# A hybrid decoder step on one core: the gate's up-unit formed before the value's, the short convolution's outer factor multiplied last, weight loads in the matching order

## The reference

```
def causal_dwconv(v, buf, w):                      # width 3, along the sequence
    cat = jnp.concatenate([buf, v], axis=1)
    return sum(w[k] * cat[:, k:k + seq] for k in range(3)), cat[:, -2:]

def short_conv_mixer(h, buf, w_in, conv_w, w_out):
    gate_b, gate_c, v = split(h @ w_in, 3)
    conv_out, new_buf = causal_dwconv(gate_c * v, buf, conv_w)
    return (gate_b * conv_out) @ w_out, new_buf

def conv_ffn(h, buf, w_up, conv_w, conv_b, w_down):
    conv_out, new_buf = causal_dwconv(h @ w_up, buf, conv_w)
    val, gate = split(conv_out + conv_b, 2)
    return (jax.nn.gelu(gate) * val) @ w_down, new_buf
```

## Time and profile before

| | |
|---|---|
| median of 3 runs | 2626.61 us (2625.88 to 2627.5) |
| the profiled execution | 2623.26 us, of which its span 2621.5 us |
| mean granted TensorE clock | 0.971 |
| PE busy | 2459.7 us (94%), 15940 matmuls |
| PEld busy | 2345.7 us (89%) |
| DVE busy | 1591.4 us (61%) |
| POOL busy | 1088.2 us (42%) |
| ACT busy | 644.4 us (25%) |
| DMA | 200.96 MB, mean 77 GB/s |

### The profile page before, as it was taken

The page is one execution under the profiler, slowest core; times in us unless marked ns, Lnnn a source line. Parts: engine busy times, 40 slices in busy tenths (PEclk is TensorE's granted clock), DMA queues, the critical chain, the costliest instruction groups (busy, mean ns, idle before and its releaser), DMA issues.

```text
span 2621.5 us, 40061 instructions
## 1 busy us (share of the span) xinstructions
PE 2459.7 (94%) x15940; PEld 2345.7 (89%) x15940; DVE 1591.4 (61%) x2224; ACT 644.4 (25%) x1255; POOL 1088.2 (42%) x770
## 2 busy tenths in 40 slices
PE   5977779998999999999998999988999999999996
PEld 2766669997999999999987999987999999999995
DVE  7766882356566666666665454656566666666665
ACT  2222341135222222212224101015312222122223
POOL 3576003455544443443444444424743444344330
PEclk8889889999999999999999999999999999999998
DMA  8666753100111111111111111101111111111102
GB/s 314 252 221 242 249 190 131 42 29 28 58 49 49 49 41 49 46 44 49 49 33 33 62 38 52 49 25 33 57 41 49 49 45 44 49 44 46 41 25 72
DMA packets 79071, 200.96 MB, mean 77 GB/s; under 512 B 27328, under 2 KB 35264, under 8 KB 77760
## 3 DMA queue, kind: packets, MB, share of 16 engines
q1 hardware_dynamic: 61952, 155.83, 17.4%
q10 hardware_dynamic: 16960, 42.80, 4.7%
HBM read 177.47 MB, written 21.14 MB: 76 GB/s over the span
## 4 chain that ended last, share of the span: by engine, by line
PE 63%; DVE 14%; issue 7%; DVEq 5%; POOL 4%; ACT 4%; POOLq 1%; DMA 1%; ACTq 0%; SPq 0%
PE bank L602 12%; PE bank L604 12%; PE bank L603 12%; PE bank L837 7%; PE bank L839 7%; PE bank L838 7%; DVEq L1846 3%; DVE ROWS L1845 3%; DVE ROWS L1844 2%; PE bank L880 1%; DVE ROWS L1848 1%; POOL WL L424 1%; DVE ROWS L1853 1%; DVE GL L1831 1%; ACT XRAW L1191 1%
## 5 line engine op out<-in xcount | busy, mean ns | idle before, releaser
L602 PE MATMUL bank<-HH,WH 128*128 128x344 f32 x3024 | 976.8, 323 | 15.2 <-ACT ROWS L1249 10.7
L603 PE MATMUL bank<-HL,WH 128*128 128x344 f32 x3024 | 969.2, 320 | 0.0
L604 PE MATMUL bank<-HH,WL 128*128 128x344 f32 x3024 | 969.0, 320 | 0.0
L422 POOL TENSOR_TENSOR WH<-RAW,ZERO 128x1024 fp32r<-128x1024 f32 x188 | 365.6, 1945 | 1149.1 <-PE bank L604 606.5
L602 PEld LDWEIGHTS bank<-HH,WH 128*128 128x128 f32 x3024 | 571.7, 189 | 30.2 <-issue 23.9
L603 PEld LDWEIGHTS bank<-HL,WH 128*128 128x128 f32 x3024 | 571.3, 189 | 0.0
L604 PEld LDWEIGHTS bank<-HH,WL 128*128 128x128 f32 x3024 | 571.2, 189 | 0.0
L424 POOL TENSOR_TENSOR WL<-RAW,WH 128x1024 fp32r<-128x1024 f32 x188 | 532.6, 2833 | 14.8
L1700 DVE SCALAR_TENSOR_TENSOR X<-bank,MOD,X 128x344 f32<-128x344 f32 (+1 forms) x480 | 274.1, 571 | 324.3 <-PE bank L839 224.1
L837 PE MATMUL bank<-GH,WH 128*128 128x344 f32 x1248 | 409.2, 328 | 14.8 <-DVE X L1724 14.7
L839 PE MATMUL bank<-GH,WL 128*128 128x344 f32 x1248 | 401.5, 322 | 0.0
(11 more groups left out here) (309 smaller groups left out, 2344.7 us busy)
## 6 DMA issues: line engine op xcount, KB each, us to landing
RAW<-in_wstream SPq DMA_DIRECT2D x188, 512.0 KB, 3.3
ADA<-in_wada ACTq DMA_DIRECT2D x40, 1024.0 KB, 5.2
s_pack<-PKA SPq DMA_DIRECT2D x8, 1344.0 KB, 4.6
PKB<-s_pack SPq DMA_DIRECT2D x12, 512.0 KB, 6.0
PKB<-s_pack SPq DMA_DIRECT2D x8, 576.0 KB, 5.0
XRAW<-in_xT SPq DMA_DIRECT2D x8, 516.0 KB, 16.6
X<-in_xT SPq DMA_DIRECT2D x1, 4128.0 KB, 13.5
out_yT<-X SPq DMA_DIRECT2D x3, 1376.0 KB, 5.6
```

Source lines behind the costliest of these rows:

```text
L422: pool.tensor_tensor(WH[:, slot, :], RAW[:, slot % 2, :], bc(ZERO[:, :], [128, 1024]), ALU.add).then_inc(s_hi, 1)
L602: pe.matmul(o, wh, hh, start=k == 0, stop=False)
L603: pe.matmul(o, wh, hl, start=False, stop=False)
L604: m = pe.matmul(o, wl, hh, start=False, stop=k == KC - 1)
```

## The change

In each ConvFFN chunk the gate's unit comes first and the value's second, on SP, PE, ACT and DVE alike. ACT waits for the split of the chunk before only in front of the value's rows. s_conv is signalled after the gate's taps, in front of the value's, and a drain stands in front of the product. In the last chunk the takes of items 0 and 1 move from between the two convolutions to the middle of the value's (behind its first tap and the drain). In the short convolution the units come in the order C, v, b. DVE begins when C and v have been copied and waits for b in front of the last product; ACT waits for s_g2 in front of the first chunk alone. The host's stream keeps its order: SP picks the units of a group in the new order with an offset, and its loop is written by phase.

```diff
+GATE_FIRST = (1, 0, 3, 2)
+B_LAST = (1, 2, 0, 4, 5, 3)
-            def load_unit(n, slot):
+            def load_unit(n, slot, at=0):
                 sp.wait_ge(s_unit, n - 1)
-                sp.dma_start(RAW[:, slot, :], wstream[bass.ds(n, 1), :, :].rearrange("a p n -> p (a n)"))\
+                sp.dma_start(RAW[:, slot, :], wstream[bass.ds(n + at, 1), :, :].rearrange("a p n -> p (a n)"))\
                     .then_inc(s_raw[slot], 16)
+            def load_phase(n0, order, groups):
+                up_n = len(order)
+                def ups(n):
+                    for q in range(up_n):
+                        load_unit(n + q, q % 2, order[q] - q)
+                ups(n0)
+                with sp.Fori(0, groups - 1) as a:
+                    ups(n0 + up_n + (up_n + 2) * a)
+                    for q in range(2):
+                        load_unit(n0 + 2 * up_n + (up_n + 2) * a + q, q)
+                for q in range(2):
+                    load_unit(n0 + up_n + (up_n + 2) * (groups - 1) + q, q)
-            with sp.Fori(14, NU // 2) as a:
-                for b in range(2):
-                    load_unit(2 * a + b, b)
+            load_phase(N_F0, GATE_FIRST, FC // 2)
+            load_phase(N_SC, B_LAST, 4)
+            load_phase(N_F1, GATE_FIRST, FC // 2)
...
# ACT, ffn_rows
-                act.wait_ge(s_g2, rows_done)
-                for vg in range(2):
+                for i, vg in enumerate((1, 0)):
+                    if first or vg == 0:
+                        act.wait_ge(s_g2, rows_done)
-                        act.wait_ge(s_up, 3 * u + 2 * t + vg + 1 if first else 3 * (u + vg) + t + 1)
-                        b = BK[3 * vg + t]
+                        act.wait_ge(s_up, 3 * u + 2 * t + i + 1 if first else 3 * (u + i) + t + 1)
+                        b = BK[3 * i + t]
...
# ACT, short_conv
-                        if q == 0:
-                            act.wait_ge(s_g2, c0 + c)
+                        if q == 0 and c == 0:
+                            act.wait_ge(s_g2, c0)
-                            dst = (T1[:, TH * t:TH * (t + 1)], U0[:, 2 + TH * t:2 + TH * (t + 1)],
-                                   U1[:, 2 + TH * t:2 + TH * (t + 1)])[q]
+                            dst = (U0[:, 2 + TH * t:2 + TH * (t + 1)], U1[:, 2 + TH * t:2 + TH * (t + 1)],
+                                   T1[:, TH * t:TH * (t + 1)])[q]
...
# DVE, ffn_conv
-                for vg in range(2):
-                    if vg and between:
-                        between()
+                for i, vg in enumerate((1, 0)):
-                    dve.wait_ge(s_ev, 3 * (u0 + 1 + vg) + 6 * cc)
+                    dve.wait_ge(s_ev, 3 * (u0 + 1 + i) + 6 * cc)
                     stt(Tr[:, 0:SEQ], Ur[:, 1:1 + SEQ], cw[1], Tr[:, 0:SEQ], M, A)
                     stt(Tr[:, SEQ:NT], st[1], cw[1], Tr[:, SEQ:NT], M, A)
                     fence()
+                    if vg == 0 and between:
+                        between()
                     stt(Tr[:, SEQ:NT], st[0], cw[0], Tr[:, SEQ:NT], M, A)
                     last = stt(Tr[:, 0:SEQ], Ur[:, 0:SEQ], cw[0], Tr[:, 0:SEQ], M, A)
-                last.then_inc(s_conv, 1)
+                    if vg == 1:
+                        last.then_inc(s_conv, 1)
             def ffn_product(cc, gel0):
+                fence()
                 dve.wait_ge(s_gelu, gel0 + 1 + cc)
...
# DVE, short_conv
-                    dve.wait_ge(s_ev, 3 * (u0 + 3 * c + 3))
+                    dve.wait_ge(s_ev, 3 * (u0 + 3 * c + 2))
...
+                    dve.wait_ge(s_ev, 3 * (u0 + 3 * c + 3))
                     tt(T0, T0, T1, M).then_inc(s_prod, 1)
```

More of the change, by code:

```diff
@@ L393, in _ @@
             sp.dma_start(STF[:, :, :, :], stf[0]).then_inc(s_late, 16)
-            with sp.Fori(0, 4) as a:
+            with sp.Fori(0, 3) as a:
                 for b in range(4):
                     load_unit(12 + 4 * a + b, b % 2)
-            with sp.Fori(14, NU // 2) as a:
-                for b in range(2):
-                    load_unit(2 * a + b, b)
+            load_phase(N_F0, GATE_FIRST, FC // 2)
+            load_phase(N_SC, B_LAST, 4)
+            load_phase(N_F1, GATE_FIRST, FC // 2)
             sp.wait_ge(s_y2, 1)
```

## The result

| | before | changed |
|---|---|---|
| median of 4 runs | 2627.06 us (2625.88 to 2628.66) | 2602.28 us (2599.6 to 2607.21) |
| profiled execution, of which span | 2623.26, 2621.5 us | 2607.21, 2605.4 us |

The ratio is 0.9907 with a 95% interval of 0.989 to 0.9925: 24.8 us faster by the medians. The profiled execution happens to be the slowest of the four, 4.9 us over their median, while that of the kernel before lies 3.8 under its own.

The account below looks back on a forecast made before the run. PE was taken as the bound, busy 594.67 of 600 us in the first ConvFFN's loop. Gains of 15.0 (loops) and 9.7 (short convolution's tail) less 2.0 (ConvFFN tails) gave 22.7 us, so 2603.9 us, range 2597 to 2614.

Parts of the forecast that it names:

- ConvFFN loops, 15.0 us: Both ConvFFN loops: 18 PE stalls for the copy of an up third vanish, a gain of 15.0 us.
- the bad bound: Short convolution's tail: the last product takes up to 2.54 us in place of 1.23 if it meets POOL.
- the 2.7 us of lower clock: Short convolution's tail: the 7.0 us PE wait lowers the clock for 6.2 us, costing 2.7 us more.
- Short convolution's tail, 9.7 us: Short convolution's tail: the 7.0 us PE wait and the lower clock behind it go, a gain of 9.7 us.
- ConvFFN tails, a loss of 1 us each: Both ConvFFN tails: the value's first taps delay the first take, costing about 1 us each, 2.0 in both.
- The wait of 0.7 before item 6: ConvFFN tails: second, 0.7 us part of PE's split wait, for the second pair of taps and take 2.
- the rival that was given 0.1: ConvFFN tails: the clock falls, 2.7 us more lost in each, gain only 17.3 us, 2609.3; chance 0.1.
- 4.4 us for both tails with POOL out of the way: ConvFFN tails: without POOL the item 6 stall vanishes, gaining 4.4 us; rival total 29.3 us, 2597.3, chance 0.1.
- Loads and drains: Whole kernel: SP's extra address arithmetic is hidden; 44 new drains cost about 0.2 us each on DVE, already counted.
- the rival that PE's waits are made up for later: The change does nothing that counts, as in layer norms behind the tails: 2624 to 2627 us; chance 0.04.
- the one in which the loop's stall stays: ConvFFN loops: the chain is no shorter where it counts; gain 7.7 us, 2618.9; chance 0.07.
- The slower rival: ConvFFN loops: DVE's chain grows by two more meetings with POOL per group, 24 us slower, 2651; chance 0.04.

Follow-up runs that it names:

- the two experiments: The changed kernel with only GELU hidden behind the value's taps, and with only the wait for the previous chunk's split moved: 2601.21 and 2601.49 us.
- the part alone: Short convolution's new unit order alone, ConvFFNs as in the kernel before: 2615.83 us, ratio 0.9962 to the kernel before.
- the kernel with only the hidden GELU: The changed kernel, but ACT waits for the previous chunk's split in front of the gate's rows, as before the change: 2601.21 us.
- the later split: The changed kernel, but POOL splits each ConvFFN's last unit only after DVE has taken tail item 3: 2604.37 us, ratio 0.9912 to before.
- the constants had been moved as well: The changed kernel with POOL's last split later and the layer norm's five constants formed before the last two chunks' work: 2596.52 us, ratio 0.9885.

## Why the prediction came out

Predicted 2603.9 us (2597 to 2614), measured 2602.28.

- **ConvFFN loops, 15.0 us**: measured 7.32 + 7.35 = 14.7, and the mechanism as written: taps at the same times, the product at their end, the copy free 2.5 us earlier, where the forecast had 2.3 (746.5 in place of 748.78). What the prediction did not say is that each half of the edit would have done alone; the two experiments showed it, and the prediction's own rows gave it (0.95 and 1.23 against 0.79).
- **Short convolution's tail, 9.7 us**: measured 10.0. The idle time and the lower clock after it are both gone, though the product did take the 2.54 us of the bad bound. That the 2.7 us of lower clock belong to the wait is shown by the part alone: with the order of before the granted clock in this tail is 0.92, with the new one 1.00.
- **ConvFFN tails, a loss of 1 us each**: +1.06 in the first, right as a figure, but by luck. Its parts were mis-sized. The wait before item 4 was 2.21 (forecast 2.3), since the taps took 4.2 us as worked out from the loop's rows. The wait of 0.7 before item 6 did not come in the first tail (in the second it was 0.13); instead the clock fell there, the rival that was given 0.1, 15 matmuls in 3.5 us, which is 3.5 - 15 x 0.158 = 1.1 us at that place and not 2.7. What the taps cost and what the clock costs come apart in the kernel with only the hidden GELU, whose first tail has the same order of taps and takes but a clock of 1.00: 58.87 us. So of the 1.06, 0.53 are the taps' and 0.53 the clock's (the rest of the 1.1 falls where that kernel waits 0.13 and 0.23 us for DVE before items 6 and 8, and the changed one does not). In the second tail the clock stayed up behind the same 2.21 us, and the cost at the full clock is again 0.53 us (73.49 against 72.96, above), not 1. There the stretch to the end reads -0.3 because the clock had fallen in the kernel before, for 1.0 us: the prediction read from the earlier trace rows that the wait of 2.02 us leaves the clock up, which is so in the first tail and was not in the second.
- **POOL's part in the tail**: the taps were long because of POOL, shown by the later split (1.28 and 0.22 us). The gain that the prediction put on it, 4.4 us for both tails with POOL out of the way, was not there until the constants had been moved as well; then it was 2.4 + 2.2 = 4.6 us. What that price had left out is that the split, moved away from the taps, lands on other work of DVE.
- **Loads and drains**: at no cost, as said; the drain in front of the product is 0.14 us.
- The layer norms behind the tails kept what they were given, so the rival that PE's waits are made up for later is out; likewise the one in which the loop's stall stays. The slower rival needed two more meetings with POOL in each group. The odd chunk's taps, behind the takes, took the same 16.7 us. The even chunk's did not: in a group before, one of them met POOL (3.06 us for 1.28), in a group of the changed kernel two do (8 sample columns in 1.86 us for 0.21 and in 2.29 for 0.23). From the first ConvFFN's third up unit to its first tail item DVE is busy 459 us where it was 432, with as many instructions, and PE has no wait for it. So "the same times as now" held for the chunk that PE had waited for, and not for DVE as a whole.

The median lies 1.6 us under the forecast; the profiled stretches sum to 24.2 us where the forecast has 22.7, and of the 1.5 us between them 1.3 are the second tail: 0.5 for the taps in place of 1.0, the 1.0 of lower clock in the kernel before, and 0.2 the other way behind the wait for ACT.

## What to carry to other kernels

When an engine that is the bound waits for the end of a chain, work out how much too long the chain is before shortening it: 0.8 us were missing here, and either of two edits gave them. A factor that is only multiplied in at the end should be computed last, so that everything before it is done while it is being computed; this pays where the chain's end is exposed, in a tail. In a tail served by one busy engine, moving its tasks about mostly moves the wait (0.3 and 0.6 us were won by it here). Find the take that PE waits for and clear what stands in front of it: the same five constants were worth nothing while the wait stood in front of them and 1.7 to 2.1 us once it stood behind. After each move, see what a split of another engine now falls beside.

## What the hardware showed unexpectedly

- A wait of about 2 us does not decide PE's clock by its size: behind the same 2.21 us it fell in the changed kernel's first tail (15 matmuls in 3.5 us) and stayed in the second. Over the six kernels with that wait in both tails it fell in 5 of 12; in the first tail it fell in four of the six and stayed in two, which run the same code there (59.40 and 58.87 us). A gain or loss of 0.5 to 1 us read from one profiled tail may be only this.
- Stretches with the same code take two lengths. The last GLU units with the layer norm and the first two units take 103.54 to 103.57 us or 105.22 to 105.27 us in the twelve traces of this study, with the same granted clock of 0.95 in the two kinds (before 103.5, changed 105.2). The windows of the traces tell them apart: the lower level comes equally long, but in the short kind behind a PE wait of 2.3 us for X, where the slower matmuls only eat into the next wait, for ACT in the layer norm (1.6 us), and in the long kind behind that wait (3.2 us), on matmuls that the layer norm needs. Before, the granted clock is 0.53 at 597.6 to 601.2 us of the span and 1.00 at 606.0 to 609.6; changed, it is 1.00 at 604.0 to 607.6 and 0.53 at 612.5 to 616.1. Why it falls behind the one wait or the other stays open.
- A DVE instruction of 8 columns takes 0.15 to 0.23 us alone and mostly 1.4 to 2.4 beside POOL's split, among them one with a single data tensor (L1703 of the kernel with the later split, 2.16 us). The Trainium skill (SBUF — State Buffer, SBUF: two separate sides) has GpSimd and VectorE exclude each other on a shared port pair for a whole instruction when VectorE reads two SBUF tensors or runs in a two-port mode. The trace agrees that the small instruction ends with POOL's; which mode L1703 runs in, it does not show. An 8-column sum that reads one of its operands from PSUM (L1741 of the changed kernel) takes 0.15 us though it starts while POOL is splitting, in all four cases.
